# Stick-breaking attention: block C taken head by head, block B's high part moved to VectorE, and some steps of the memory attention put elsewhere

## The chip, the core and the metric

The kernel runs on one core of a Trainium2 chip. The core has five engines with instruction queues of their own: TensorE (PE: matmuls, with PEld for its weight loads), VectorE (DVE), ScalarE (ACT), GpSimd (POOL) and SyncE (SP, which issues the DMAs). They meet only through semaphores. The metric is the device time of one execution in microseconds, and lower is better. Each engine works through its own list in order, so an instruction that waits holds up all that stand behind it on its engine.

## The reference

A streaming encoder with two layers over 512 tokens of width 1024, all in float32. Layer 0 has a half SwiGLU block, a mixer of gated spatial weights and a memory cross-attention of four heads, and a second half SwiGLU block. Layer 1 has the same blocks, but its mixer is stick-breaking attention over a shared K and V (12 heads of 64) beside the memory cross-attention. The change is in the two mixers. Stick-breaking attention in the reference, cut to the core:

```python
z = einsum('bqhd,bkhd->bhqk', qi, k) * scale
causal = key_pos < qpos
log_beta = log_sigmoid(z)
log_one_minus = where(causal, log_sigmoid(-z), 0.0)
suffix = cumsum(log_one_minus, reverse=True) - log_one_minus   # over the keys
a = where(causal, exp(log_beta + suffix), 0.0)
out = einsum('bhqk,bkhd->bqhd', a, v)
```

Memory cross-attention is plain softmax attention over 256 memory rows, four heads of 64.

## The kernel before

Every float32 product is made of three matmuls in a fast number format: each operand is split into a high part (a rounded copy, written by ScalarE or VectorE) and a low part (what the rounding lost, a subtraction, mostly on GpSimd). Names end in `_hi` and `_lo`. All weights stream through two buffers: SyncE loads `raw`, ScalarE writes `w_hi`, GpSimd writes `w_lo`, TensorE multiplies. One such piece of weights is a unit (`unit_T`, `unit_N`, `unit_wide`).

The kernel has no scheduler. The order on each engine is the order of the code, written by hand in five blocks, one for each engine. Small steps that don't use the weight stream are put between the matmuls of a unit as its `steps`: `unit_T` runs step 0 after two of its eight k-chunks, step 1 after four, step 2 after six and step 3 at the end. The memory attention runs in this way. For each head h there are `mem_scores`, `mem_transposes` and `mem_values` on TensorE, and `mem_steps` says which stands where.

The stick-breaking attention of layer 1 goes over six pairs of heads (`PAIRS`, index c). Keys lie on partitions and queries along the columns, in blocks of 128 keys. These are grouped in three: A holds key blocks 1 and 3, B holds block 2, C holds block 0. A and C have 2 x 512 columns for the two heads of a pair, B has 2 x 256. For each of A, B and C of a pair the work is a chain through all engines:

1. TensorE: the dots z (`sb_scores_a`, `_b`, `_c`), with the causal mask.
2. VectorE: the absolute value (`sb_abs`) into `sp_l`. ScalarE: `sb_exp` and `sb_log` in place, log(1 + exp(-|z|)). VectorE: `sb_plus` adds max(z, 0). This is the softplus of z.
3. The high part `sp_hi` (`sb_high`, on VectorE for A and C; `sb_high_b`, on ScalarE, for B from pair 1 on), then the low part `sp_lo` on GpSimd (`sb_low`, `lows_after`).
4. TensorE: the sums over later keys, as matmuls with a triangle (`tri_r`) or minus ones (`minus_r`), added to z in the same PSUM bank (`sb_sums_a_high`, `sb_sums_a_low`, `sb_sums_b`, `sb_sums_b_on_a`, `sb_sums_c`).
5. ScalarE: `sb_out`, the exponential, which gives the weights `aT`. TensorE: `sb_values` multiplies them with V; then `sb_y` splits the result into `y_hi` and `y_lo`.

The chains of several pairs overlap. TensorE in round c (the body of its loop for pair c) runs the sums of A and B of pair c, the values of pair c-1 around the scores of B of pair c+1, the sums of C of pair c, the scores of C of pair c+1 and the scores of A of pair c+2. PSUM is full: the scores of A of pair c+2 go into the banks of C of pair c, and so wait for its `aT_c` (`s_a[C_]`). The scores of B of pair c+1 use the one bank of B and wait for `aT_b` of pair c (`s_a[B_]`). `sp_hi_c` and `sp_lo_c` have one buffer each; those of A and B have two. The last pair's sums of C and its values run as steps of the output projection.

The semaphores that the change touches are `s_sp`, `s_sphi`, `s_splo`, `s_tri` (the sums of a block are complete) and `s_a`.

## Time and profile before

| | before |
|---|---|
| median of 3 runs | 1857.85 us (1857.71 to 1858.12) |
| the profiled execution | 1858.24 us |
| its span in the trace | 1856.5 us |
| TensorE busy | 1848.3 us |
| GpSimd, VectorE, ScalarE busy | 902.7, 842.1, 639.9 us |
| granted TensorE clock | full speed in all 40 slices |

The span is the time between the first and the last instruction of the trace; the time of an execution is a little longer. Busy times count the time in which an engine had an instruction at work. The attention over the six pairs lies between about 1364 and 1448 us of the span; the memory attention of layer 0 between about 415 and 456 us, and that of layer 1 between about 1339 and 1383 us.

### The profile page before, as it was taken

What the parts mean: (1) busy time and instruction counts of PE and PEld (TensorE: products, weight loads), DVE (VectorE), ACT (ScalarE), POOL (GpSimd) and SP (SyncE); (2) the same over time, 40 slices, a digit from 0 to 9 for tenths busy, and PEclk for the clock granted to TensorE, in tenths of its full rate; (3) what the DMA queues carried; (4) which work ended last, traced back from release to release, by engine and by line L of the source; (5) the groups of instructions that cost most, each with busy time, mean ns of one, the idle gap of its engine ahead of it and who ended that gap; (6) DMA issues with size and microseconds to landing.
All of it is one profiled execution on the core that took longest, in us unless ns stands there. A gap on an engine that the chain in (4) does not pass through costs nothing.

```text
span 1856.5 us, 22737 instructions
## 1 busy us (share of the span) xinstructions
PE 1848.3 (100%) x8640; PEld 1527.7 (82%) x8640; DVE 842.1 (45%) x723; ACT 639.9 (34%) x894; POOL 902.7 (49%) x433
## 2 busy tenths in 40 slices
PE   9999999999999999999999999999999999999999
PEld 7888888897888888888888888888877888888887
DVE  7442154554555520554435530444667455502543
ACT  6432232336443221323333222223568333222223
POOL 5444444563444544444545444544658445444542
PEclk9999999999999999999999999999999999999999
DMA  6223322352232234223322223222310232233222
GB/s 205 91 83 96 115 90 67 114 171 74 69 112 92 85 85 125 90 74 96 124 92 90 93 82 119 91 87 82 107 65 1 75 107 90 75 106 113 90 71 88
DMA packets 215981, 175.56 MB, mean 95 GB/s; under 512 B 3247, under 2 KB 212989, under 8 KB 215933
## 3 DMA queue, kind: packets, MB, share of 16 engines
q1 hardware_dynamic: 215932, 174.90, 30.2%
q8 instruction: 32, 0.52, 0.1%
q14 instruction: 17, 0.13, 0.0%
HBM read 172.79 MB, written 2.10 MB: 94 GB/s over the span
## 4 chain that ended last, share of the span: by engine, by line
PE 98%; ACT 1%; DVE 0%; DMA 0%; POOL 0%; issue 0%; SPq 0%; ACTq 0%
PE ps L591 31%; PE ps L592 31%; PE ps L593 31%; PE ps L899 1%; PE ps L1016 1%; PE ps L663 1%; PE ps L690 1%; PE ps L892 1%; PE ps L860 0%; PE ps L872 0%; PE ps L881 0%; PE ps L1073 0%; DMA x_in<-in_x_dram 0%; ACT aT_c L1508 0%; PE ps L794 0%; PE ps L1160 0%
## 5 line engine op out<-in xcount | busy, mean ns | idle before, releaser
L483 POOL TENSOR_TENSOR w_lo<-raw,w_hi 128x1024 fp32r<-128x1024 f32 (+2 forms) x360 | 824.9, 2312 | 908.6 <-ACT w_hi L1221 908.6
L1221 ACT ACTIVATE w_hi<-raw 128x1024 fp32r<-128x1024 f32 (+2 forms) x361 | 328.6, 958 | 1097.8 <-PE ps L593 1089.9
L591 PE MATMUL ps<-u_hi,w_hi 128*128 128x512 f32 x1568 | 612.3, 390 | 0.0
L592 PE MATMUL ps<-u_lo,w_hi 128*128 128x512 f32 x1568 | 610.8, 390 | 0.0
L593 PE MATMUL ps<-u_hi,w_lo 128*128 128x512 f32 x1568 | 610.7, 389 | 0.0
L591 PEld LDWEIGHTS ps<-u_hi,w_hi 128*128 128x128 f32 x1568 | 294.4, 188 | 61.9 <-issue 0.6
L593 PEld LDWEIGHTS ps<-u_hi,w_lo 128*128 128x128 f32 x1568 | 294.4, 188 | 61.4
L592 PEld LDWEIGHTS ps<-u_lo,w_hi 128*128 128x128 f32 x1568 | 294.5, 188 | 60.6 <-issue 0.2
L591 PE MATMUL ps<-mid_hi,w_hi 128*128 128x512 f32 (+1 forms) x714 | 276.2, 387 | 0.0
L593 PE MATMUL ps<-mid_hi,w_lo 128*128 128x512 f32 (+1 forms) x714 | 275.9, 386 | 0.0
L592 PE MATMUL ps<-mid_lo,w_hi 128*128 128x512 f32 (+1 forms) x714 | 275.9, 386 | 0.0
L1584 DVE TENSOR_TENSOR mid_lo<-t_mid,mid_hi 128x512 f32 (+1 forms) x88 | 176.9, 2049 | 54.1 <-ACT mid_hi L1275 54.1
L1584 DVE TENSOR_TENSOR t_up<-t_gate,rinv 128x512 f32<-128x512 f32 x88 | 166.2, 1927 | 57.2 <-ACT t_gate L1268 57.2
L1721 DVE SCALAR_TENSOR_TENSOR xT<-ps,xT 128x512 f32 (+1 forms) x63 | 43.6, 692 | 276.5 <-PE ps L593 276.5
L592 PEld LDWEIGHTS ps<-mid_lo,w_hi 128*128 128x128 f32 x714 | 134.1, 188 | 27.1
L593 PEld LDWEIGHTS ps<-mid_hi,w_lo 128*128 128x128 f32 x714 | 134.1, 188 | 27.0
L591 PEld LDWEIGHTS ps<-mid_hi,w_hi 128*128 128x128 f32 x714 | 134.1, 188 | 26.9
L1584 DVE TENSOR_TENSOR t_gate<-ps,rinv 128x512 f32<-128x512 f32 (+1 forms) x89 | 58.9, 703 | 194.1 <-PE ps L593 194.1
L1584 DVE TENSOR_TENSOR t_mid<-ps,t_up 128x512 f32<-128x512 f32 x88 | 56.7, 686 | 178.1 <-PE ps L593 177.7
L1584 DVE TENSOR_TENSOR ssq<-ssq,sq 128x512 f32<-128x512 f32 x52 | 99.8, 1920 | 12.7 <-ACT sq L1251 12.2
L1590 DVE SCALAR_TENSOR_TENSOR u_lo<-xT,gains,u_hi (+1 forms) x40 | 39.5, 986 | 48.3 <-ACT u_hi L1249 48.3
L1268 ACT ACTIVATE t_gate<-t_gate 128x512 f32<-128x512 f32 x88 | 50.1, 616 | 11.3 <-DVE t_gate L1584 11.3
(252 smaller groups left out, 1363.6 us busy)
## 6 DMA issues: line engine op xcount, KB each, us to landing
raw<-in_ffn_w_up_dram SPq DMA_DIRECT2D x44, 1024.0 KB, 5.3
raw<-in_ffn_w_gate_dram SPq DMA_DIRECT2D x43, 1024.0 KB, 5.3
raw<-in_ffn_w_down_dram SPq DMA_DIRECT2D x32, 768.0 KB, 4.8
raw<-in_ffn_w_down_dram SPq DMA_DIRECT2D x32, 640.0 KB, 4.4
raw<-in_a_w_in_dram SPq DMA_DIRECT2D x7, 1024.0 KB, 5.3
raw<-in_w_kv_dram SPq DMA_DIRECT2D x6, 1024.0 KB, 5.0
raw<-in_a_w_out_dram SPq DMA_DIRECT2D x4, 1024.0 KB, 5.1
raw<-in_b_w_in_dram SPq DMA_DIRECT2D x4, 1024.0 KB, 5.4
```

The costliest lines, as they stand in the source:

```text
L483: nc.gpsimd.tensor_tensor(w_lo[:, n % 2, part], raw[:, n % 2, part], w_hi[:, n % 2, part].bitcast(F32), ALU.subtract).then_inc(s_wlo, 1)
L591: nc.tensor.matmul(dst, s_hi, m_hi_, start=first, stop=False)
L592: nc.tensor.matmul(dst, s_hi, m_lo_, start=False, stop=False)
L593: return nc.tensor.matmul(dst, s_lo, m_hi_, start=False, stop=last)
L663: last = nc.tensor.matmul(dst, o[:, k, toks], w[:, k, :], start=k == 0 and t % 2 == 0 and term == 0, stop=k == DK - 1 and term == 2, skip_ ...
L690: last = nc.tensor.matmul(ps[:, bank(0) + c, :], w[:, k, c * P:(c + 1) * P], u[:, k, :], start=k == 0 and w is wh and u is u_hi, stop=k == ...
L892: last = nc.tensor.matmul(dst, w[rows_, c, j * P:(j + 1) * P], m[rows_, m_k, j * P:], start=first and w is k_hi and m is q_hi, stop=False, ...
L1221: nc.scalar.activation(w_hi[:, n % 2, part], raw[:, n % 2, part], ACT.Copy).then_inc(s_whi, 1)
L1268: nc.scalar.activation(t_gate[:, q, :], t_gate[:, q, :], ACT.Silu).then_inc(s_silu, 1)
L1584: return nc.vector.tensor_tensor(dst, x, y, op)
L1590: nc.vector.scalar_tensor_tensor(u_lo[:, bass.ds(i + k, 1), :], xT[:, bass.ds(i + k, 1), :], gains[:, bass.ds(i + (gain + k), 1)], u_hi[:, ...
L1721: nc.vector.scalar_tensor_tensor(x_k, ps[:, bank(n):bank(n) + 1, :], 0.5, x_k, ALU.mult, ALU.add).then_inc(s_evac, 1)
```

## The change

Stick-breaking attention, block C:
- `sb_plus` and `sb_high` of C become `sb_plus_and_high_c`, which takes head 0 and then head 1, 512 columns each. `sb_low_c` does the same for the low part. `s_sp`, `s_sphi` and `s_splo` of C count to two for each pair.
- `sb_sums_c` runs the triangle matmuls as high and low of head 0, then high and low of head 1, with a new semaphore `s_tri_c0` for head 0. It waits for both heads' `s_sp` at its start.
- `sb_out_c` takes the exponential of head 0 after `s_tri_c0` and that of head 1 after `s_tri`.

Block B: its logarithm (`sb_log`) moves behind `sb_out_c` on ScalarE. Its high part moves from ScalarE to VectorE for all pairs, and stands there between `sb_plus(B_)` and `sb_abs(C_)`.

Values of pair 4 (`c == PAIRS - 2`): the wait for `aT_c` moves from the start of `sb_values` to block C's matmuls, the last of the four.

Memory attention: `mem_scores` of head 1 moves by one slot, to stand directly before the transposes of head 0, in both layers. In layer 0 the transposes of the spatial weights follow the values of head 3 directly, mixes 0 and 1 run two k-chunks later in their unit, mixes 2 and 3 directly behind them (so in the unit before their old one), and mixes 4 and 5 stay.

```diff
@@ gpsimd
+            def sb_low_c(c):
+                for e in range(2):
+                    pool.wait_ge(s_sphi[C_], 2 * c + e + 1)
+                    nc.gpsimd.tensor_tensor(sp_lo[C_][c % 2][:, e, :], sp_l[C_][:, e, :],
+                                            sp_hi[C_][c % 2][:, e, :].bitcast(F32),
+                                            ALU.subtract).then_inc(s_splo[C_], 1)
@@ tensor
             def sb_sums_c(c):
-                pe.wait_ge(s_sp[C_], c + 1)
+                pe.wait_ge(s_sp[C_], 2 * c + 2)
...
-                pe.wait_ge(s_sphi[C_], c + 1)
-                for e in range(2):
+                for e, done in enumerate((s_tri_c0, s_tri[C_])):
+                    pe.wait_ge(s_sphi[C_], 2 * c + e + 1)
                     add_high(z[:, e, :], tri_r[:], C_, c, e, WHOLE)
-                pe.wait_ge(s_splo[C_], c + 1)
-                for e in range(2):
-                    last = add_low(z[:, e, :], tri_r[:], C_, c, e, WHOLE)
-                last.then_inc(s_tri[C_], 1)
+                    pe.wait_ge(s_splo[C_], 2 * c + e + 1)
+                    add_low(z[:, e, :], tri_r[:], C_, c, e, WHOLE).then_inc(done, 1)
 
             def sb_values(c, blocks):
                 first, end = (1, 0) if c == PAIRS - 2 else (0, TT - 1)
-                for x in (A_, B_, C_):
+                for x in (A_, B_) if c == PAIRS - 2 else (A_, B_, C_):
                     pe.wait_ge(s_a[x], c + 1)
...
+                    if c == PAIRS - 2 and x == C_:
+                        pe.wait_ge(s_a[x], c + 1)
@@ mem_steps
-                        scores(1), transposes(0), both(values(0), scores(2)), transposes(1),
+                        nothing, both(scores(1), transposes(0)), both(values(0), scores(2)), transposes(1),
@@ layer 0
-            unit_T(n + 4, ... steps=(lambda: mem_values(0, 3), spatial_weights, nothing, nothing))
-            unit_T(n + 5, ... steps=(nothing, mixes(0), nothing, nothing))
-            unit_T(n + 6, ... steps=(nothing, mixes(2), nothing, mixes(4)))
+            unit_T(n + 4, ... steps=(values_and_weights, nothing, nothing, nothing))
+            unit_T(n + 5, ... steps=(nothing, nothing, lambda: mixes(range(4)), nothing))
+            unit_T(n + 6, ... steps=(nothing, nothing, nothing, lambda: mixes(range(4, GK))))
@@ scalar
-            def sb_high_b(c):
...
+            def sb_out_c(c):
+                if c:
+                    act.wait_ge(s_bv, c)
+                for e, ready in enumerate((s_tri_c0, s_tri[C_])):
+                    act.wait_ge(ready, c + 1)
+                    last = nc.scalar.activation(aT[C_][c % 2][:, e, :], ps_of(C_, c)[:, e, :], ACT.Exp)
+                last.then_inc(s_a[C_], 1)
...
                     sb_exp(B_, c + 1)
-                    sb_log(B_, c + 1)
...
-                sb_out(C_, c)
+                sb_out_c(c)
                 if more:
-                    sb_high_b(c + 1)
+                    sb_log(B_, c + 1)
                     sb_exp(C_, c + 1)
                     sb_log(C_, c + 1)
@@ vector
+            def sb_plus_and_high_c(c):
+                dve.wait_ge(s_ln[C_], c + 1)
+                for e in range(2):
+                    nc.vector.scalar_tensor_tensor(sp_l[C_][:, e, :], ps_of(C_, c)[:, e, :], 0.0, sp_l[C_][:, e, :],
+                                                   ALU.max, ALU.add).then_inc(s_sp[C_], 1)
+                    dve.wait_ge(s_sp[C_], 2 * c + e + 1)
+                    if c:
+                        dve.wait_ge(s_tri[C_], c)
+                    nc.vector.tensor_copy(sp_hi[C_][c % 2][:, e, :], sp_l[C_][:, e, :]).then_inc(s_sphi[C_], 1)
...
-                sb_plus(C_, c)
-                sb_high(C_, c)
+                sb_plus_and_high_c(c)
...
                     sb_plus(B_, c + 1)
+                    sb_high(B_, c + 1)
                     sb_abs(C_, c + 1)
```

ScalarE's list around the exponential of block C, pair 2, before. The first `sp_l_b` is the exponential of B of pair 3 and the second its logarithm; the numbers behind the names tell two buffers of one name apart, and the semaphores waited for stand in brackets:

```order
L1508 ACTIVATE aT_a_126<-ps 128x1024 [waits s_bv,s_tri_a]
L1495 ACTIVATE sp_l_b<-sp_l_b 128x512 [waits s_abs_b]
L1500 ACTIVATE sp_l_b<-sp_l_b 128x512 [waits s_em_b]
L1508 ACTIVATE aT_c_130<-ps 128x1024 [waits s_bv,s_tri_c]
L1515 ACTIVATE sp_hi_b_117<-sp_l_b 128x512 [waits s_tri_c,s_sp_b]
L1495 ACTIVATE sp_l_c<-sp_l_c 128x1024 [waits s_abs_c]
L1500 ACTIVATE sp_l_c<-sp_l_c 128x1024 [waits s_em_c]
L1508 ACTIVATE aT_b_129<-ps 128x512 [waits s_bv,s_tri_b]
```

The same place in the changed kernel:

```order
L1522 ACTIVATE aT_a_126<-ps 128x1024 [waits s_bv,s_tri_a]
L1509 ACTIVATE sp_l_b<-sp_l_b 128x512 [waits s_abs_b]
L1530 ACTIVATE aT_c_130<-ps 128x512 [waits s_tri_c0,s_bv]
L1530 ACTIVATE aT_c_130<-ps 128x512 [waits s_tri_c]
L1514 ACTIVATE sp_l_b<-sp_l_b 128x512 [waits s_em_b]
L1509 ACTIVATE sp_l_c<-sp_l_c 128x1024 [waits s_abs_c]
L1514 ACTIVATE sp_l_c<-sp_l_c 128x1024 [waits s_em_c]
L1522 ACTIVATE aT_b_129<-ps 128x512 [waits s_bv,s_tri_b]
```

The logarithm of B has moved behind `aT_c`, which is now two instructions, and the copy `sp_hi_b` is gone from ScalarE.

VectorE's list from the high part of A of pair 2 to the absolute value of B of pair 3, before:

```order
L1952 CAST sp_hi_a_114<-sp_l_a 128x1024 [waits s_tri_c,s_sp_a]
L1584 TENSOR_TENSOR y_lo<-ps,y_hi 128x512 [waits s_byhi]
L1943 SCALAR_TENSOR_TENSOR sp_l_b<-ps,sp_l_b 128x512 [waits s_ln_b]
L1937 TENSOR_SCALAR sp_l_c<-ps 128x1024 [waits s_splo_c,s_z_c]
L1937 TENSOR_SCALAR sp_l_a<-ps 128x1024 [waits s_splo_a,s_z_a]
L1943 SCALAR_TENSOR_TENSOR sp_l_c<-ps,sp_l_c 128x1024 [waits s_ln_c]
L1952 CAST sp_hi_c_118<-sp_l_c 128x1024 [waits s_tri_c,s_sp_c]
L1937 TENSOR_SCALAR sp_l_b<-ps 128x512 [waits s_splo_b,s_z_b]
```

The same stretch in the changed kernel:

```order
L1966 CAST sp_hi_a_114<-sp_l_a 128x1024 [waits s_tri_c,s_sp_a]
L1599 TENSOR_TENSOR y_lo<-ps,y_hi 128x512 [waits s_byhi]
L1958 SCALAR_TENSOR_TENSOR sp_l_b<-ps,sp_l_b 128x512 [waits s_ln_b]
L1966 CAST sp_hi_b_116<-sp_l_b 128x512 [waits s_tri_c,s_sp_b]
L1952 TENSOR_SCALAR sp_l_c<-ps 128x1024 [waits s_splo_c,s_z_c]
L1952 TENSOR_SCALAR sp_l_a<-ps 128x1024 [waits s_splo_a,s_z_a]
L1972 SCALAR_TENSOR_TENSOR sp_l_c<-ps,sp_l_c 128x512 [waits s_ln_c]
L1977 CAST sp_hi_c_118<-sp_l_c 128x512 [waits s_tri_c,s_sp_c]
L1972 SCALAR_TENSOR_TENSOR sp_l_c<-ps,sp_l_c 128x512
L1977 CAST sp_hi_c_118<-sp_l_c 128x512 [waits s_tri_c,s_sp_c]
L1952 TENSOR_SCALAR sp_l_b<-ps 128x512 [waits s_splo_b,s_z_b]
```

The cast of B is new between B's sum and C's absolute value, and the sum and cast of C are each in two halves that alternate.

## Rows read from the trace of the kernel before

**Rows 1.** The page's part 1: each engine's busy time and instructions.
```profile
PE 1848.3 (100%) x8640; PEld 1527.7 (82%) x8640; DVE 842.1 (45%) x723; ACT 639.9 (34%) x894; POOL 902.7 (49%) x433
```
**Rows 2.** Busy times by window, memory attention of both layers: window, length, engines, clock.
```profile
414.00:500.00 86.00, 85.96 (x480) 70.12 (x479) 41.56 (x44) 45.00 (x81) 30.50 (x12) 1.00 0.26 83
1338.00:1372.00 34.00, 34.00 (x209) 26.59 (x208) 17.03 (x17) 18.67 (x46) 20.36 (x8) 1.00 0.25 82
```
**Rows 3.** The same view of rounds 2 and 3 (PE, PEld, DVE, ACT, POOL).
```profile
1400.71:1411.63 10.92, 10.86 (x71) 7.82 (x71) 8.56 (x10) 9.04 (x11) 8.71 (x8) 1.00 0.01 2
1411.63:1422.54 10.91, 10.84 (x71) 7.83 (x71) 8.56 (x10) 9.02 (x11) 8.70 (x8) 1.00 0.00 0
```
**Rows 4.** Waits: who waited for whom, us in total, times, longest.
```profile
PEld ps L892 <- ACT aT_c L1508: 2.0, 4, 0.5
...
PE ps L899 <- POOL sp_lo_c L505: 0.7, 1, 0.7
...
PE ps L1016 <- ACT aT_c L1508: 0.3, 1, 0.3
```
**Rows 5.** Timeline of TensorE, round 4: start, duration, instruction, count.
```profile
1422.07 0.40 PE L892 MATMUL ps<-q_lo_rest,k_hi 64*128 64x512 f32 x2
1422.54 0.44 PE L892 MATMUL ps<-q_hi,k_hi 64*128 64x384 f32 x2
...
1427.50 0.38 PE L892 MATMUL ps<-q_hi,k_hi 64*128 64x256 f32 x1
...
1431.25 0.62 PE L899 MATMUL ps<-sp_hi_c,tri_r 128*128 128x512 f32 x2
```
**Rows 6.** Timeline of ScalarE, from B's logarithm to `aT_b` and A's exponential.
```profile
1420.94 0.64 ACT L1500 ACTIVATE sp_l_b<-sp_l_b 128x512 f32<-128x512 f32 x1
1421.48 1.00 ACT L1508 ACTIVATE aT_c<-ps 128x1024 f32<-128x1024 f32 x1
...
1423.81 1.06 ACT L1495 ACTIVATE sp_l_c<-sp_l_c 128x1024 f32<-128x1024 f32 x1 [0.50 <-DVE sp_l_c L1937]
1424.90 1.06 ACT L1500 ACTIVATE sp_l_c<-sp_l_c 128x1024 f32<-128x1024 f32 x1
1425.96 0.60 ACT L1508 ACTIVATE aT_b<-ps 128x512 f32<-128x512 f32 x1
1426.45 1.05 ACT L1495 ACTIVATE sp_l_a<-sp_l_a 128x1024 f32<-128x1024 f32 x1
```
**Rows 7.** Chain of what ended last, pair 0's block C: start, duration, what.
```profile
1383.47 1.23 DVE sp_l_c L1943
1384.73 0.70 DVE sp_hi_c L1952
1385.50 2.39 POOL sp_lo_c L505
1387.94 0.75 PE ps L899 x2
```
**Rows 8.** Timelines of VectorE and GpSimd: casts of 512 columns, and GpSimd's work.
```profile
1379.21 0.92 DVE L1952 CAST sp_hi_b<-sp_l_b 128x512 fp32r<-128x512 f32 x1
...
543.69 0.43 DVE L1600 CAST ssq_hi<-ssq 128x512 fp32r<-128x512 f32 x1
...
1377.45 2.39 POOL L505 TENSOR_TENSOR sp_lo_a<-sp_l_a,sp_hi_a 128x1024 fp32r<-128x1024 f32 x1 [6.43 <-DVE sp_hi_a L1952]
...
1383.48 1.28 POOL L557 TENSOR_TENSOR lo<-sp_lo_a,lo 128x512 fp32r<-128x512 f32 x1
```
**Rows 9.** Timelines of VectorE and GpSimd, round 3.
```profile
1421.96 0.68 DVE L1943 SCALAR_TENSOR_TENSOR sp_l_b<-ps,sp_l_b 128x512 f32<-128x512 f32 x1
1422.56 1.22 DVE L1937 TENSOR_SCALAR sp_l_c<-ps 128x1024 int32<-128x1024 int32 x1
...
1421.52 2.39 POOL L505 TENSOR_TENSOR sp_lo_a<-sp_l_a,sp_hi_a 128x1024 fp32r<-128x1024 f32 x1 [1.45 <-DVE sp_hi_a L1952]
```
**Rows 10.** Chain of what ended last, layer 0: scores of memory head 1.
```profile
422.16 0.90 PE ps L860 x12
```

More of the change, by code:

```diff
@@ L307, in trunk_program @@
         s_zb0 = sem("s_zb0")
+        s_tri_c0 = sem("s_tri_c0")
         s_lo23, s_lo123 = sem("s_lo23"), sem("s_lo123")
@@ L563, in _ @@
             for c in range(PAIRS):
-                sb_low(C_, c)
+                sb_low_c(c)
                 if c + 1 < PAIRS:
@@ L1081, in _, with values_and_weights, mixes @@
             unit_wide(n + 2, u_hi, u_lo, steps=steps[4:])
-            unit_T(n + 4, 0, u_hi, u_lo, steps=(lambda: mem_values(0, 3), spatial_weights, nothing, nothing))
-            def mixes(g):
-                return lambda: (mix(g), mix(g + 1))
-            unit_T(n + 5, 0, u_hi, u_lo, steps=(nothing, mixes(0), nothing, nothing))
-            unit_T(n + 6, 0, u_hi, u_lo, steps=(nothing, mixes(2), nothing, mixes(4)))
+            def values_and_weights():
+                mem_values(0, MH - 1)
+                spatial_weights()
+            unit_T(n + 4, 0, u_hi, u_lo, steps=(values_and_weights, nothing, nothing, nothing))
+            def mixes(groups):
+                for g in groups:
+                    mix(g)
+            unit_T(n + 5, 0, u_hi, u_lo, steps=(nothing, nothing, lambda: mixes(range(4)), nothing))
+            unit_T(n + 6, 0, u_hi, u_lo, steps=(nothing, nothing, nothing, lambda: mixes(range(4, GK))))
             def y_ready_a(k):
@@ L1508, in sb_out @@
                 nc.scalar.activation(aT[x][c % 2][:], ps_of(x, c), ACT.Exp).then_inc(s_a[x], 1)
-            def sb_high_b(c):
-                act.wait_ge(s_sp[B_], c + 1)
-                if c > 1:
-                    act.wait_ge(s_tri[C_], c - 1)
-                nc.scalar.activation(sp_hi[B_][c % 2][:], sp_l[B_][:], ACT.Copy).then_inc(s_sphi[B_], 1)
+            def sb_out_c(c):
[5 more added lines that the diff above has]
+                last.then_inc(s_a[C_], 1)
             def sb_y(c):
@@ L1935, in sb_abs @@
                 if c:
-                    dve.wait_ge(s_splo[x], c)
+                    dve.wait_ge(s_splo[x], 2 * c if x == C_ else c)
                 nc.vector.tensor_scalar(sp_l[x][:].bitcast(I32), ps_of(x, c).bitcast(I32), 0x7FFFFFFF, None,
@@ L1948, in sb_high @@
                 dve.wait_ge(s_sp[x], c + 1)
-                used = c if x == C_ else c - 1
-                if used > 0:
-                    dve.wait_ge(s_tri[C_], used)
+                if c > 1:
+                    dve.wait_ge(s_tri[C_], c - 1)
                 nc.vector.tensor_copy(sp_hi[x][c % 2][:], sp_l[x][:]).then_inc(s_sphi[x], 1)
+            def sb_plus_and_high_c(c):
[7 more added lines that the diff above has]
+                    nc.vector.tensor_copy(sp_hi[C_][c % 2][:, e, :], sp_l[C_][:, e, :]).then_inc(s_sphi[C_], 1)
             def sb_y(c):
```

## The prediction, as made before the changed kernel was run

> **What bounds the kernel now.** The page is read first. TensorE is busy for 1848.3 of 1856.5 us, VectorE for 842.1, ScalarE for 639.9 and GpSimd for 902.7 [rows 1]. Every microsecond of TensorE is therefore on the path, and work on the other three costs nothing until TensorE waits for it. The change touches two stretches. In the memory attention of both layers TensorE is busy for 85.96 of 86 us and for all of 34 us [rows 2], so nothing is there to win: the scores and transposes only change places in it. The other stretch is the stick-breaking loop, a few us in each of five rounds. A round takes 10.92 us, of which VectorE works 8.6, ScalarE 9.0 and GpSimd 8.7 [rows 3]: three helpers at four fifths, which hand data to each other in a fixed order.
>
> The list of waits comes next, and it names all that the change can win [rows 4]. Once TensorE waits 0.7 us for the low half of block C's softplus (pair 0). Four times the weight load of `sb_scores_a` waits for `aT_c`, 2.0 us by the list; but a load normally runs ahead of its matmul, so the cost is smaller. The matmul rows give it: the last group of block C's dots starts at 1422.07 and the next at 1422.54, 0.47 us later, where its 512 columns take 0.23 [rows 5]. So each of these stalls costs 0.24 us. Last, `sb_values(4)` waits 0.3 us for the same `aT_c`. Together 0.7 + 4 x 0.24 + 0.3 = 1.9 us, 0.1% of the time.
>
> **The change, part by part.**
>
> *Block C's exponential by head.* TensorE now finishes head 0 (its high and low matmul) before it starts head 1, so ScalarE starts 0.46 us earlier. A 512-column exponential holds ScalarE for 0.49 us (1425.96 to 1426.45) and takes 0.60; the 1024-column one takes 1.00 [rows 6]. The end moves from 1.00 after the last sum to 0.6, which is 0.4 earlier and more than the stall of 0.24. The matmuls are as many as before, of the same size. Alone, this would remove the stalls in rounds 1 to 4.
>
> *Block C's softplus and high part by head, pair 0.* Now: sum 1383.47, cast 1384.73, subtraction 1385.50 for 2.39 us, matmul 1387.94 [rows 7]. What matters is how a VectorE cast meets GpSimd. A cast of 512 columns alone takes 0.43 us. At 1379.21 the cast of `sp_hi_b` took 0.92: GpSimd had been on `sp_lo_a` since 1377.45 for 2.39 us, to 1379.84, and the cast ended at 1380.13, 0.29 later [rows 8]. So it stood still until GpSimd's instruction was over. Applied to pair 0: sum of head 0 to 1384.15; its cast waits for GpSimd's `lo` (1383.48 to 1384.76, rows 8), ends 1385.05; subtraction of head 0 at 1385.12 to 1386.41 (GpSimd takes 1.28 for 512 columns, rows 8); sum of head 1 ends 1385.65 (`sb_sums_c` now waits for it first, within the same stall); its cast stands until 1386.41 and ends at 1386.70; subtraction of head 1 ends at 1388.06; matmul at 1388.12. Only one 0.23 matmul is left then instead of two, so it is done at 1388.35 against 1388.40 now. Gain: nothing. The 0.7 us stall stays, since the casts and subtractions of the two heads cannot overlap.
>
> *The logarithm of block B behind `aT_c`, its cast on VectorE.* This makes a loop through all engines that did not bind before. I count from the moment when TensorE has finished head 0 of block C of one round. Exponentials of both heads: 0.07 to start, 0.49 each: 1.05. Logarithm of B 0.63: 1.68 [rows 6]. VectorE's sum for B 0.68: 2.39, cast ready to start at 2.42 [rows 9]. Where is GpSimd? The subtraction `sp_lo_a` starts 1.20 us after TensorE began the high sums of block C (1421.52 against 1420.32, the latter being 1431.25 less one round of 10.93), which is 0.58 on my clock, and lasts 2.39: to 2.97 [rows 5, 9]. The cast of B stands behind it and ends at 3.26. Behind the cast in VectorE's order waits the absolute value of block C of the next pair, which now runs at 1422.56, straight behind B's sum [rows 9]. It starts at 3.2, ends at 4.40. Exponential of C 4.43, logarithm 1.09 later, 5.52; `aT_b` 6.5 (it followed 1.06 behind the logarithm, where it may have waited a little; I take 1.0), 0.60 long: 7.1; TensorE may start `sb_scores_b` at 7.2 [rows 6]. From that start to head 0's end TensorE needs 1431.25 - 1427.50 = 3.75, plus 0.23 and 0.39: 4.37 [rows 5]. The loop is 7.2 + 4.35 = 11.55 us, against 10.92 now: 0.63 a round. The new wait is `sb_scores_b` for `aT_b`; today it has almost 1 us to spare (ready 1426.56, used 1427.50 [rows 5, 6]). Queued behind it on ScalarE are A's exponential and logarithm, which move back by the same time but are needed only 3 us later.
>
> ScalarE's cast of B (about 0.6 us) goes away; it is worth nothing, since the loop's delay is on VectorE.
>
> The Trainium skill, "SBUF — State Buffer", section "Who interferes with whom", says that copy, cast and tensor_scalar can all take the port pair that VectorE shares with GpSimd, and that the second to come is blocked wholly. For the cast the trace agrees (0.92 against 0.43). For the absolute value, a tensor_scalar out of PSUM, it does not: it took 1.22 at 1422.56 in the midst of `sp_lo_a`, as elsewhere. By the rule read so widely C's absolute value would stand behind `sp_lo_b` too, and the round would be over 12.5 us; the row decides, and I leave it out.
>
> *First round and pair 1.* The same walk from pair 0: head 1 of C ends at 1388.5, ScalarE's second half at 1389.06, logarithm of B to 1389.69, sum to 1390.40; `sp_lo_a` now runs 1389.23 to 1391.62, so the cast ends 1391.9, C's absolute value 1393.05, `aT_b` 1395.74, `sb_scores_b` 1395.80. Now it starts at 1394.74 (1427.50 less three rounds of 10.92 [rows 3, 5]); the cost is 1.1 us. Pair 1 also carries `query_rest_low(1)`, a VectorE subtraction with both inputs in SBUF, in the same crowded place. No row shows it there behind a blocked cast: between 0 and 0.7 us (its own length), I take 0.3.
>
> *Values of pair 4 per block.* Blocks A and B go first and hide `aT_c`: the stall of 0.3 goes, and so does the 0.24 in the last `sb_scores_a`, as the loop has made ScalarE early there.
>
> *Memory scores beside transposes; mixes and spatial weights moved.* Same matmuls, two to three us earlier or later in weights work without a wait. Scores of head 1 take 0.90 [rows 10]; what follows them (maximum, exponential) must wait for the transposes of head 0 in any case, because both use `pm`. I price this at 0, with 0.1 us on either side for each of the four places, a tenth of a 0.9 us step.
>
> **Sum.** 1.1 + 3 x 0.63 + 0.3 - 0.5 = 2.8 us. The profiled execution took 1858.24 us with its span of 1856.5; with 2.8 more that is 1861.0. The median of the runs is 0.39 lower, so the forecast for it is 1860.6.
>
> **Rivals.**
> *It does what it says.* The stalls of 1.9 us go and nothing new comes: 1856.0. For it: ScalarE and VectorE have over 2 us free in a round. Against it: that spare time lies elsewhere than between B's logarithm and C's absolute value, and the casts stand. Chance 0.13.
> *The cast of B does not stand.* If A's subtraction is over or not yet begun when B's cast comes, the cast takes 0.43 from 2.42, and C's absolute value starts at 2.8 instead of 3.2: a loop of 11.15 us, 0.2 a round. With a first round at no cost and 0.5 won at the end, the sum is about zero: 1857.8. Chance 0.15.
> *GpSimd becomes the bound, clearly slower.* Its halves cost 2 x 1.29 for 2.39, and each cast of block C waits for the half before it. This pushes A's absolute value, sum and subtraction back too. It decides from the point where the second half of C ends later than TensorE asks for it (in round 0 it does). Then `sp_lo_a` and `sp_lo_b` come late and the round is 12.1 us: 4 x 1.2 - 0.5 = 4.3 us, 1862.2. Chance 0.14.
> *Forecast*: chance 0.58, own range 1859.3 to 1861.7.
>
> **How the numbers follow.** Range 1857.2 to 1862.2: below it lies the first rival (0.13), above it half of the third (0.07). About 0.2%, 3.7 us, is what a measurement of this kernel can tell from no change. Faster by that needs 1854.1, more than all stalls together: 0.01. Slower by that needs 1861.6: most of the third rival and the forecast's upper end, 0.17. The rest, 0.82, is within.
>
> **What would show it.** In the changed profile: casts of `sp_hi_b` of 0.7 to 1.5 us that end 0.29 after `sp_lo_a`; C's absolute value more than 2.5 us behind head 0's end; TensorE waiting for `aT_b` (line of `sb_dots`) in rounds 1 to 4; rounds of about 11.5 us; the wait at 1387 still there; no wait for `aT_c` in `sb_scores_a` or `sb_values`; the two memory stretches as long as before. I am wrong if the rounds are at or under 10.9 us, or if B's casts take 0.43.

## The result and the profile after

| | before | after |
|---|---|---|
| median of 20 runs each | 1857.86 us (1857.57 to 1860.01) | 1860.57 us (1860.18 to 1861.53) |
| profiled execution, span | 1858.24, 1856.5 us | 1860.19, 1858.5 us |

The ratio is 1.0015, with a 95% interval of 1.0009 to 1.0021: the change costs 2.7 us, and 1860.6 had been forecast. Engine times hardly moved, as the page's part 1 of the changed kernel shows beside [rows 1]:

```profile
PE 1849.3 (100%) x8640; PEld 1526.9 (82%) x8640; DVE 849.9 (46%) x740; ACT 636.2 (34%) x895; POOL 904.4 (49%) x439
```

TensorE's busy time rose by 1.0 us and the span by 2.0, so the shares of busy time don't tell where the time went. The list of waits of the changed kernel (attention stretch; who waited for whom, us in total, times, longest) answers to [rows 4]:

```profile
PEld ps L901 <- ACT aT_b L1522: 3.8, 4, 1.0
PEld ps L908 <- POOL sp_lo_b L506: 2.2, 4, 0.7
PE ps L908 <- POOL sp_lo_b L506: 1.4, 4, 0.4
...
PE ps L901 <- ACT aT_b L1522: 1.1, 4, 0.3
...
PEld ps L901 <- ACT aT_c L1530: 0.5, 3, 0.2
...
PEld ps L908 <- DVE sp_l_c L1972: 0.3, 1, 0.3
PE ps L908 <- POOL sp_lo_c L513: 0.3, 1, 0.3
```

The stalls for `aT_c` are nearly gone (2.0 us to 0.5, and none in the values). Two new ones took their place: TensorE waits for B's low part and then for `aT_b`, once in each of the four rounds. One round in the timeline of the changed kernel (VectorE, GpSimd, ScalarE; start, duration), to be held beside [rows 6, 9]:

```profile
1411.19 1.09 ACT L1530 ACTIVATE aT_c<-ps 128x512 f32<-128x512 f32 x2
...
1411.66 2.40 POOL L506 TENSOR_TENSOR sp_lo_a<-sp_l_a,sp_hi_a 128x1024 fp32r<-128x1024 f32 x1 [1.27 <-DVE sp_hi_a L1966]
1412.16 0.63 ACT L1514 ACTIVATE sp_l_b<-sp_l_b 128x512 f32<-128x512 f32 x1
...
1412.82 0.69 DVE L1958 SCALAR_TENSOR_TENSOR sp_l_b<-ps,sp_l_b 128x512 f32<-128x512 f32 x1 [0.64 <-ACT sp_l_b L1514]
...
1413.55 0.79 DVE L1966 CAST sp_hi_b<-sp_l_b 128x512 fp32r<-128x512 f32 x1
...
1414.26 1.21 DVE L1952 TENSOR_SCALAR sp_l_c<-ps 128x1024 int32<-128x1024 int32 x1
...
1415.51 1.06 ACT L1509 ACTIVATE sp_l_c<-sp_l_c 128x1024 f32<-128x1024 f32 x1 [2.72 <-DVE sp_l_c L1952]
...
1416.60 1.06 ACT L1514 ACTIVATE sp_l_c<-sp_l_c 128x1024 f32<-128x1024 f32 x1
...
1417.56 0.58 ACT L1522 ACTIVATE aT_b<-ps 128x512 f32<-128x512 f32 x1
...
1418.19 0.18 PEld L901 LDWEIGHTS ps<-q_hi,k_hi 64*128 64x128 f32 x1 [0.96 <-ACT aT_b L1522]
```

`sp_lo_a` ends at 1414.06 and the cast at 1414.34. C's absolute value starts behind it, 1.44 us after B's sum began; it was 0.60 [rows 9]. ScalarE idles 2.72 us in front of C's exponential.

**A ruler for the rest.** Start-up differs by up to 1.3 us from one profiled execution to the next (the sums of squares in layer 0 start 25.5 to 26.8 us behind the first matmul, whatever the kernel). In the profiled execution of the changed kernel TensorE came to the attention 1.0 us earlier than in that of the kernel before, which is why the spans differ by 2.0 us and the attention by 3.0. So the traces are compared by lengths inside the attention: from the start of TensorE's first matmul of `sp_hi_c` of one pair to that of the next ("rounds" 0 to 4), and from the start of the first matmul of `q_hi,k_hi` to that of the last of `aT_c` ("attention"). What lies before round 0 and behind round 4 is in "attention" alone. The times are the medians.

| kernel | round 0, 1, 2, 3, 4 | attention | time |
|---|---|---|---|
| before | 11.88 10.93 10.91 10.93 11.08 | 82.37 | 1857.85 to 1858.02 |
| after | 12.54 11.96 11.48 11.47 10.73 | 85.33 | 1860.57 |
| 1 memory steps alone | 11.90 10.92 10.91 10.92 11.07 | 82.36 | 1857.49 |
| 2 C by head alone | 11.80 11.14 10.98 10.99 11.14 | 83.05 | 1858.55 |
| 3 after, B's high part on ScalarE | 11.80 11.50 10.98 10.97 10.74 | 83.01 | 1858.18 |
| 4 after, B's logarithm first | 12.55 11.95 11.47 11.48 10.75 | 85.34 | 1860.54 |
| 5 B's high part on VectorE alone | 12.20 11.47 11.47 11.47 11.08 | 84.58 | 1860.13 |
| 6 C's exponential by head alone | 11.82 10.97 10.99 10.98 11.14 | 82.53 | 1858.36 |
| 7 after, B's high part without a cast | 11.85 11.46 11.37 11.37 10.73 | 83.87 | 1859.01 |
| 8 first candidate | 11.68 10.98 10.98 10.98 10.74 | 83.71 | 1858.67 |
| 9 memory steps and values | 11.89 10.93 10.92 10.91 10.74 | 82.02 | 1857.13 |
| 10 B's high part behind C's absolute value | 12.02 11.14 11.15 11.14 11.07 | 83.15 | 1858.71 |
| 11 as 6, B's logarithm behind | 12.13 11.24 10.98 10.97 10.74 | 82.81 | 1858.27 |
| 12 as 8, sums wait by head | 11.17 10.97 10.97 10.97 10.73 | 81.97 | 1857.06 |

Each experiment's time is a median of 11 runs; the kernel before ran beside them, 1858.02, 1857.93, 1857.85 and 1857.87 us in the four sets (1 to 4, 5 to 8, 9 to 11, 12). The intervals of the ratios are about 0.0009 wide on either side. So by the medians alone only the changed kernel and experiments 4 and 5 are slower for certain, and differences under 1.7 us rest on the rounds.

### The profile page after: what moved, and what is told of

It reads as the page before. It is cut to its first block, busy times and chain, and to the rows that moved or that the text cites. A ratio compares the mean times of both kernels' runs of the same rounds, so it can differ in the third digit from the quotient of the medians.

```text
span 1858.5 us, 22765 instructions
## 1 busy us (share of the span) xinstructions
PE 1849.3 (100%) x8640; PEld 1526.9 (82%) x8640; DVE 849.9 (46%) x740; ACT 636.2 (34%) x895; POOL 904.4 (49%) x439
## 4 chain that ended last, share of the span: by engine, by line
PE 97%; DVE 1%; ACT 1%; POOL 1%; issue 1%; DVEq 0%; POOLq 0%
PE ps L600 31%; PE ps L601 31%; PE ps L602 31%; PE ps L672 1%; PE ps L699 1%; POOL sp_lo_a L506 1%; PE ps L908 0%; PE ps L869 0%; PE ps L1025 0%; PE ps L881 0%; DVE sp_l_c L1952 0%; PE ps L890 0%; DVE sp_l_a L1958 0%; PE ps L1082 0%; ACT sp_l_c L1509 0%
```

## The experiments

**1. The memory steps alone.**

```diff
-                        scores(1), transposes(0), both(values(0), scores(2)), transposes(1),
+                        nothing, both(scores(1), transposes(0)), both(values(0), scores(2)), transposes(1),
...
+            unit_T(n + 4, 0, u_hi, u_lo, steps=(values_and_weights, nothing, nothing, nothing))
```

> The kernel before with the changes to the memory attention and the mixes alone; the stick-breaking part is as before. My prediction (priced at nothing): 0.0 us, within 0.1 for each of the four places. What the start times of the matmuls in the changed kernel's trace say instead: -0.1 us at the memory attention of layer 0, -0.1 at the mixes, -0.1 at the memory attention of layer 1, -0.35 together, so a median of 1857.5 against 1857.9. If TensorE's list around these steps has a cost when it goes back and forth between them and the weight matmuls, the gain stays; if it was chance, the three places show no shift.

1857.49 beside 1858.02 us; ratio 0.9998 (0.9989 to 1.0007). Counted from the sums of squares in layer 0, TensorE gains 0.13 us over the memory scores of layer 0, 0.10 over its values and mixes, and 0.12 in layer 1: 0.35, with the attention as long as before. The gain is real, and the changed kernel has the same one: from the sums of squares to the attention it is 1336.56 to 1336.62 us in the eight traces with these steps and 1336.92 to 1336.95 in the six without. Part of where it comes from shows in the chain (start, duration, line; L591 to L593 are the weight matmuls, L860 the scores, L872 the transposes). Before:

```profile
423.06 0.43 PE ps L591
...
426.05 0.87 PE ps L872 x8
426.93 0.23 PE ps L591
```

With scores and transposes beside each other:

```profile
424.46 0.90 PE ps L860 x12
425.36 1.02 PE ps L872 x8
426.38 0.23 PE ps L591
```

The weight matmul behind the scores took 0.43 us and takes 0.23 elsewhere; the transposes behind the scores take 1.02 for 0.87. That is 0.05 of the 0.13; where the rest is, these rows don't tell.

**2. Block C by head alone**, with B as before.

```diff
 # on the kernel before
+                    add_high(z[:, e, :], tri_r[:], C_, c, e, WHOLE)
+                    pe.wait_ge(s_splo[C_], 2 * c + e + 1)
+                    add_low(z[:, e, :], tri_r[:], C_, c, e, WHOLE).then_inc(done, 1)
...
+                sb_plus_and_high_c(c)      # VectorE
+                sb_low_c(c)                # GpSimd
+                sb_out_c(c)                # ScalarE
```

> The kernel before with block C by head alone (softplus, high and low part, sums, exponential); block B's logarithm stays ahead of aT_c and its high part on ScalarE; pair 4's values and the memory steps as before. Theory (the loop through B's cast is the cost): most of the change's +3.0 us in the attention is absent here; left is a later round 0 and the blocked second cast, about +1.0 us, rounds of 10.9 to 11.1. Rival (GpSimd's and VectorE's halves are the cost): +2 us or more, with rounds of over 11.3. Rival (it does what it says): -1 to -2 us.

1858.55 us, ratio 1.0003 (0.9994 to 1.0012); attention +0.68. The rounds are 10.98 to 11.14, so GpSimd's halves are not the bound. But nothing is gained either: TensorE's weight loads still wait 2.1 us for `aT_c`. C's cast of head 0 stands behind GpSimd in four of the six pairs, for 1.53 to 1.55 us.

**3. The changed kernel with B's high part back on ScalarE.**

```diff
                     sb_log(B_, c + 1)
+                    sb_high_b(c + 1)
...
                     sb_plus(B_, c + 1)
-                    sb_high(B_, c + 1)
```

> The changed kernel with block B's high part back on ScalarE, directly behind B's logarithm (which stays behind aT_c). Theory (the cast of B on VectorE stands until GpSimd's sp_lo_a ends and pushes C's absolute value): C's absolute value starts straight behind B's sum again, rounds fall from 11.5 to 11.0 or less, and the time from 1860.6 to about 1858.1 (+0.2 to +0.5 over before). Rival (the late logarithm of B is the cost): 1860 or more, and the wait of sb_scores_b for aT_b stays at over 0.3 us a round.

1858.18 us, ratio 1.0001 (0.9992 to 1.0010); attention 83.01, which gives back 2.32 of the 2.96 us. C's absolute value starts at 1412.88, 0.61 behind the start of B's sum (1412.27), and rounds 2 and 3 are 10.98 and 10.97. Most of the cost is thus the cast on VectorE; round 1 stays at 11.50, for 10.93 before.

**4. The changed kernel with B's logarithm first.**

```diff
                     sb_exp(B_, c + 1)
+                    sb_log(B_, c + 1)
...
-                    sb_log(B_, c + 1)
                     sb_exp(C_, c + 1)
```

> The changed kernel with block B's logarithm back ahead of aT_c; its high part stays on VectorE. Theory (the blocked cast): B's sum comes earlier but its cast ends with sp_lo_a all the same, so C's absolute value is no earlier: within 0.3 us of the changed kernel, 1860.6, rounds of 11.4 to 11.5. Rival (the late logarithm of B is the cost, two thirds of the loop's delay): 1858.5, rounds of 11.0.

1860.54 us, ratio 1.0014 (1.0005 to 1.0023), and every round within 0.02 us of the changed kernel's. In this kernel it is nothing that the logarithm stands behind `aT_c`.

**5. B's high part on VectorE alone.** On the kernel before:

```diff
-                    sb_high_b(c + 1)
...
                     sb_plus(B_, c + 1)
+                    sb_high(B_, c + 1)
                     sb_abs(C_, c + 1)
```

> The kernel before with one edit: block B's high part on VectorE between B's sum and C's absolute value, from ScalarE. Theory (this cast stands until GpSimd's sp_lo_a ends and holds C's absolute value back): this edit alone costs most of the change's 2.95 us in the attention, about +2.4 us: 1860.3, rounds of about 11.4, and sb_scores_b waits for aT_b. Rival (the cost needs block C by head or the late logarithm of B beside it): under +1 us, 1858.9 or less.

1860.13 us, ratio 1.0013 (1.0004 to 1.0022); attention +2.21. Rounds 2 and 3 are 11.47, the same as in the changed kernel to 0.01; rounds 0 and 1 are 0.34 and 0.49 shorter than there. Its timeline:

```profile
1411.13 2.39 POOL L505 TENSOR_TENSOR sp_lo_a<-sp_l_a,sp_hi_a 128x1024 fp32r<-128x1024 f32 x1 [1.01 <-DVE sp_hi_a L1944]
1411.57 0.68 DVE L1935 SCALAR_TENSOR_TENSOR sp_l_b<-ps,sp_l_b 128x512 f32<-128x512 f32 x1
...
1412.29 1.52 DVE L1944 CAST sp_hi_b<-sp_l_b 128x512 fp32r<-128x512 f32 x1
1413.73 1.21 DVE L1929 TENSOR_SCALAR sp_l_c<-ps 128x1024 int32<-128x1024 int32 x1
```

The cast begins 1.16 us behind the start of `sp_lo_a`, where it was 1.89 in the changed kernel, takes 1.52 for 0.79, and ends 0.29 after `sp_lo_a` (1413.81, 1413.52), for 0.28 there. Where a cast stands behind GpSimd, its own start is worth nothing; GpSimd's end decides. That is also why experiment 4 showed no difference.

**6. C's exponential by head alone**, softplus and parts whole.

```diff
+                for e, done in enumerate((s_tri_c0, s_tri[C_])):
+                    pe.wait_ge(s_sphi[C_], c + 1)
+                    add_high(z[:, e, :], tri_r[:], C_, c, e, WHOLE)
+                    pe.wait_ge(s_splo[C_], c + 1)
+                    add_low(z[:, e, :], tri_r[:], C_, c, e, WHOLE).then_inc(done, 1)
...
+                sb_out_c(c)
```

> The kernel before with block C's sums and exponential by head alone; its softplus, high and low part stay whole. My prediction said that this alone removes the four stalls of sb_scores_a for aT_c (-1.0 us: 1857.0), since ScalarE starts 0.46 us earlier. Rival, by the rows before: ScalarE is not free earlier, as B's exponential and logarithm stand ahead (the logarithm ends at 1421.47, and aT_c starts at 1421.48); two exponentials of 512 then end 0.05 to 0.1 later than one of 1024, and the stalls stay at 0.5 us in the list: +0.2 to +0.3 us, 1858.2.

1858.36 us, ratio 1.0001 (0.9992 to 1.0010); attention +0.16. The rival holds. ScalarE's timeline here:

```profile
1420.98 0.62 ACT L1494 ACTIVATE sp_l_b<-sp_l_b 128x512 f32<-128x512 f32 x1
1421.63 0.63 ACT L1499 ACTIVATE sp_l_b<-sp_l_b 128x512 f32<-128x512 f32 x1
1422.17 1.06 ACT L1515 ACTIVATE aT_c<-ps 128x512 f32<-128x512 f32 x2
```

`aT_c` starts when B's logarithm is done, as before, and its two halves take 1.06 us for 1.00.

**7. B's high part without a cast.** In the changed kernel VectorE writes it with the operation of the sum, out of PSUM.

```diff
+                nc.vector.scalar_tensor_tensor(sp_hi[B_][c % 2][:], ps_of(B_, c), 0.0, sp_l[B_][:], ALU.max,
+                                               ALU.add).then_inc(s_sphi[B_], 1)
+                dve.wait_ge(s_sphi[B_], c + 1)
                 nc.vector.scalar_tensor_tensor(sp_l[B_][:], ps_of(B_, c), 0.0, sp_l[B_][:], ALU.max,
                                                ALU.add).then_inc(s_sp[B_], 1)
```

> The changed kernel, where block B's high part is written on VectorE by the operation of its sum (max(z, 0) + l, z out of PSUM, rounded on writing) and not by a cast; the sum itself follows it, and GpSimd and TensorE wait for both. VectorE so does 0.68 us where the cast took 0.43, but the operation is of a kind that did not stand behind GpSimd in the trace. Theory (the cast stands because of what it reads and writes, not because it is one more instruction): both take 0.68 each, in the midst of sp_lo_a too; C's absolute value starts earlier and the rounds are 11.1: about 1858.8. Rival (any added instruction there costs as much, or this one stands too): 1860.6 or more.

1859.01 us, ratio 1.0007 (0.9998 to 1.0016); attention 83.87, 1.46 less than the changed kernel's. Its timeline:

```profile
1410.93 2.41 POOL L508 TENSOR_TENSOR sp_lo_a<-sp_l_a,sp_hi_a 128x1024 fp32r<-128x1024 f32 x1 [1.16 <-DVE sp_hi_a L1969]
...
1411.91 0.69 DVE L1976 SCALAR_TENSOR_TENSOR sp_hi_b<-ps,sp_l_b 128x512 fp32r<-128x512 f32 x1 [0.46 <-ACT sp_l_b L1517]
1412.63 0.69 DVE L1979 SCALAR_TENSOR_TENSOR sp_l_b<-ps,sp_l_b 128x512 f32<-128x512 f32 x1
1413.24 1.21 DVE L1955 TENSOR_SCALAR sp_l_c<-ps 128x1024 int32<-128x1024 int32 x1
```

Two operations of 0.69 us pass within `sp_lo_a`, neither held. What stood in the changed kernel was the cast from SBUF to SBUF, not an added instruction as such. Kind of operation and source were changed together here, so which of the two decides is not shown. Rounds 2 and 3 fall only to 11.37 where 11.1 was expected, since a second 0.69 us takes the place of most of the stall; 1.2 of the 1.46 us come from rounds 0 and 1.

**8. A candidate**: experiment 3, with C's high parts written in the manner of 7.

```diff
+                    nc.vector.scalar_tensor_tensor(sp_hi[C_][c % 2][:, e, :], ps_of(C_, c)[:, e, :], 0.0,
+                                                   sp_l[C_][:, e, :], ALU.max, ALU.add).then_inc(s_sphi[C_], 1)
+                    dve.wait_ge(s_sphi[C_], 2 * c + e + 1)
                     nc.vector.scalar_tensor_tensor(sp_l[C_][:, e, :], ps_of(C_, c)[:, e, :], 0.0, sp_l[C_][:, e, :],
```

> The changed kernel with two edits: block B's high part back on ScalarE behind B's logarithm, and block C's high parts written by the operation of the sum out of PSUM (high, then sum, for each head; GpSimd waits for both), so that no cast of 512 columns is left that GpSimd's subtraction of the other head can hold up. Theory: the second head's high part no longer stands behind the subtraction of the first, C's low part ends earlier, the wait of pair 0 shrinks and the stalls for aT_c go: attention -1.2 us against the kernel before, with the memory steps 1856.4. Rival (the longer operations on VectorE, 0.25 us each, take back what they give): 1857.5 to 1858.

1858.67 us, ratio 1.0001 (0.9992 to 1.0010); attention +1.34, not -1.2. A miss, and most of it is in pair 0: the first `sp_hi_c` matmul comes 24.11 us into the attention, for 22.39 before, while rounds 0 to 4 together are only 0.4 us shorter. Its row in the waits, and its windows (length; busy PE, PEld, DVE, ACT, POOL; granted clock):

```profile
PE ps L909 <- DVE sp_l_c L1986: 0.7, 1, 0.7
```

```profile
1384.00:1385.00 1.00, 0.75 (x4) 0.42 (x4) 0.97 (x3) 0.97 (x2) 0.80 (x1) 1.00 0.00 0
1385.00:1386.00 1.00, 0.57 (x4) 0.57 (x4) 1.00 (x3) 1.00 (x3) 0.96 (x2) 0.88 0.00 0
1386.00:1387.00 1.00, 1.00 (x6) 1.00 (x6) 1.00 (x1) 0.83 (x2) 0.81 (x1) 0.50 0.00 0
...
1388.00:1389.00 1.00, 1.00 (x4) 0.81 (x3) 0.17 (x1) 0.42 (x1) 1.00 (x1) 0.50 0.00 0
```

TensorE waits 0.7 us for C's last sum, ahead of all the minus-one sums, and behind this wait its clock is granted at 0.50 (1.2 GHz) for some 3 us. The triangle matmuls of 512 columns follow each other every 0.43 us there, for 0.23. The eleven times lie in two groups, 1857.2 to 1857.8 (four) and 1858.2 to 1859.0 (seven). The mean granted clock of the run is 0.999 in six of the seven, the profiled one among them, and 1.000 in the four and in the seventh, 1858.24; some 3 us at 0.50 make 0.001 of the span. That the clock fell here only in the second group is therefore likely, but only the profiled run, 1858.73, shows where it fell.

In the kernel before, TensorE waits as long in pair 0 (0.7 us for the low part), and the clock stays at 1.00:

```profile
1387.00:1388.00 1.00, 0.29 (x2) 0.06 (x1) 0.97 (x2) 0.97 (x3) 0.89 (x1) 1.00 0.00 0
1388.00:1389.00 1.00, 1.00 (x6) 0.84 (x8) 1.00 (x3) 0.62 (x2) 0.48 (x1) 1.00 0.00 0
```

**9. Memory steps and pair 4's values.**

```diff
-                for x in (A_, B_, C_):
+                for x in (A_, B_) if c == PAIRS - 2 else (A_, B_, C_):
...
+                    if c == PAIRS - 2 and x == C_:
+                        pe.wait_ge(s_a[x], c + 1)
```

> The kernel before with the two parts of the change that nothing spoke against: the memory steps and mixes (0.37 us in the first experiment), and pair 4's values that wait per block (the wait of 0.3 us in the list, 0.28 by the loop as it was). Theory: the two add up: -0.65 us, 1857.3, and it beats both kernels. Rival (the wait of pair 4's values only moves to the next instruction that needs ScalarE or the sums of pair 5): 1857.6.

1857.13 us (1856.92 to 1857.66) beside 1857.85 (1857.53 to 1858.76); ratio 0.9996 (0.9987 to 1.0005). It is 0.7 us faster, as expected, and its ranges nearly don't meet, though the interval of the ratio doesn't exclude no change. In the trace round 4 is 0.34 shorter, and the wait of the values for `aT_c` is gone from the list.

**10. B's high part on VectorE, behind C's absolute value.**

```diff
                     sb_plus(B_, c + 1)
                     sb_abs(C_, c + 1)
+                    sb_high(B_, c + 1)
```

> As the experiment with block B's high part alone on VectorE (1860.1, +2.2 us), but behind C's absolute value and no longer ahead of it. The cast stays on VectorE and may still stand behind GpSimd. Theory (the price is that C's absolute value is queued behind the standing cast): C's absolute value starts straight behind B's sum, the rounds are 10.9 to 11.0 and the time is 1857.9 to 1858.2. Rival (the price is the late high and low part of B itself, or VectorE's added work): 1859.5 or more, for B's high part comes later still.

1858.71 us, ratio 1.0006 (0.9997 to 1.0015); attention +0.78, between the two. C's absolute value starts at once and B's cast is short; C's cast is the longer one:

```profile
1410.90 0.68 DVE L1935 SCALAR_TENSOR_TENSOR sp_l_b<-ps,sp_l_b 128x512 f32<-128x512 f32 x1
...
1411.50 1.21 DVE L1929 TENSOR_SCALAR sp_l_c<-ps 128x1024 int32<-128x1024 int32 x1
1412.63 0.52 DVE L1944 CAST sp_hi_b<-sp_l_b 128x512 fp32r<-128x512 f32 x1
...
1416.05 1.28 POOL L557 TENSOR_TENSOR lo<-sp_lo_a,lo 128x512 fp32r<-128x512 f32 x1
1416.19 1.68 DVE L1944 CAST sp_hi_c<-sp_l_c 128x1024 fp32r<-128x1024 f32 x1
```

So 1.4 of the 2.2 us of experiment 5 are what was queued behind the cast. The other 0.8 is the recorded rival's late low part of B. B's cast still ends 0.29 us after `sp_lo_a`, so `sp_lo_b` starts later, and TensorE waits for it:

```profile
1413.22 1.31 POOL L505 TENSOR_TENSOR sp_lo_b<-sp_l_b,sp_hi_b 128x512 fp32r<-128x512 f32 x1 [0.37 <-DVE sp_hi_b L1944]
...
1414.58 0.19 PEld L899 LDWEIGHTS ps<-sp_lo_b,tri_r 128*128 128x128 f32 x1 [0.19 <-POOL sp_lo_b L505]
```

The same two of the kernel before, where the round begins 0.15 us later (1409.42, here 1409.27):

```profile
1412.98 1.29 POOL L505 TENSOR_TENSOR sp_lo_b<-sp_l_b,sp_hi_b 128x512 fp32r<-128x512 f32 x1
...
1414.47 0.19 PEld L899 LDWEIGHTS ps<-sp_lo_b,tri_r 128*128 128x128 f32 x1
```

From the round's start `sp_lo_b` begins 0.39 us later (3.95 for 3.56), its weight load 0.26 (5.31 for 5.05), and the round is 11.15 for 10.91. C's own cast is no new stall: it took 1.27 us before, and ends 0.55 after GpSimd's `lo` in both.

**11. As 6, with B's logarithm behind `aT_c`**, B's high part on ScalarE.

```diff
                     sb_exp(B_, c + 1)
-                    sb_log(B_, c + 1)
...
+                    sb_log(B_, c + 1)
                     sb_high_b(c + 1)
```

> As the experiment with block C's sums and exponential by head alone (1858.4), and block B's logarithm moved behind aT_c, its high part still on ScalarE behind it. Theory (exponential by head gains only where ScalarE is free when head 0 is complete): the waits of sb_scores_a for aT_c, 2.1 us in the list before, go; instead TensorE waits for B's low part, about 0.15 us a round; rounds of 10.9, the attention 0 to 0.3 us shorter than in the kernel before: 1857.6 to 1857.9. Rival (the stalls for aT_c stay, because the second head's exponential ends no earlier): 1858.4 or more.

1858.27 us, ratio 1.0002 (0.9993 to 1.0011); attention +0.44. The stalls for `aT_c` go (2.0 us before and 1.7 in 6, to 0.3), so exponential by head needs the freed ScalarE. But rounds 2 and 3 are 10.98 and 10.97, no shorter. The waits moved:

```profile
PEld ps L893 <- ACT aT_b L1507: 2.4, 4, 0.6
PEld ps L900 <- POOL sp_lo_c L506: 1.9, 3, 1.3
PEld ps L900 <- POOL sp_lo_b L506: 1.3, 4, 0.4
```

Of these only the last is a new cost in rounds 2 and 3. The load in front of `sb_scores_b` idles 0.60 us a round in the kernel before too, where the list calls it "issue", and 1.3 us of the second line is the stall of pair 0, 1.1 there. The second half of the expectation was wrong: in rounds 2 and 3 TensorE waits for B's late low part as much as it gains, and in rounds 0 and 1 the kernel takes 0.3 us more each than that of 6 (12.13 and 11.24 for 11.82 and 10.97).

**12. The candidate with the wait for C's sums by head.**

```diff
-                pe.wait_ge(s_sp[C_], 2 * c + 2)
                 z = ps_of(C_, c)
                 for e in range(2):
+                    pe.wait_ge(s_sp[C_], 2 * c + e + 1)
```

> The candidate of before (B's high part on ScalarE, C's high parts by the operation of the sum), where TensorE waits for the sum of each head of C ahead of that head's minus-one sums, and no longer for both heads at the start. In the candidate's profile TensorE's granted clock fell to 0.50 (1.2 GHz) behind the wait of pair 0, from 1385.9 to 1389.1, and its times lay in two groups (4 runs from 1857.2 to 1857.8, 7 from 1858.2 to 1859.0). Theory (that wait, and the low clock behind it, are the whole miss): head 0's sums fill the wait, the clock stays at 1.00 and all runs lie about 1857.2, the attention at about 82.2. Rival (the rounds of 10.98 and the longer work on VectorE cost as much as was won): about 1857.5 with the clock at 1.00, the attention at 82.5 or more; or the wait is only split in two, and the clock falls again: 1858.5.

1857.06 us (1856.87 to 1857.69) beside 1857.87 (1857.72 to 1858.45), ratio 0.9996 (0.9987 to 1.0005); attention 81.97, 0.40 shorter than before. The theory's numbers hold: with the wait split the clock stays at 1.00 there, and 1.74 of the attention's microseconds come back. How much of them is the wait and how much the clock, this pair of runs doesn't tell. It was not the whole miss of 8, which had expected -1.2. The same stretch:

```profile
1385.00:1386.00 1.00, 0.68 (x4) 0.69 (x5) 1.00 (x3) 1.00 (x3) 0.96 (x2) 1.00 0.00 0
1386.00:1387.00 1.00, 1.00 (x6) 0.79 (x6) 0.99 (x1) 0.89 (x3) 0.71 (x1) 1.00 0.00 0
```

With 9 it is the fastest kernel here; all its 11 times lie under those of the kernel before beside them. It wins the stall of pair 0 (round 0: 11.17 for 11.88, though its first `sp_hi_c` matmul comes 22.91 us into the attention for 22.39) and the values' wait (0.34), and pays 0.05 in each of rounds 1 to 3. Experiment 9, with the memory steps and the values' wait alone, is within 0.05 us of it in the attention (82.02).

## Why the prediction was right

*The loop.* It failed nowhere. From the start of `aT_c` (1411.19, 0.07 on the prediction's clock) the changed kernel has B's cast end at 3.22 (forecast 3.26), C's absolute value at 3.14 (3.2; it starts while the cast ends), C's exponential at 4.39 (4.43), its logarithm at 5.48 (5.52), `aT_b` at 6.44 (6.5) and `sb_scores_b` at 7.07 (7.2). The round is 11.47, not 11.55: `sb_scores_b` came 0.13 early, half of it in the last step (0.63 us, where 0.7 had been taken), and from there to head 0's end it is 4.40, where the sum has 4.35 and its own working 4.37. The cause is shown both ways, by adding the cast (5) and by taking it away (3), and its kind by 7.

*First round and pair 1.* `sb_scores_b` of pair 2 starts at 1394.75, and TensorE came to the attention 1.01 us earlier than before, so it lost 1.02 against 1394.74; 1.1 was forecast. From there to its start for pair 3 are 11.97 us, then 11.47 and 11.48: +1.05, +0.55, +0.56 to 10.92, forecast 0.93, 0.63, 0.63. `query_rest_low`, put at 0.3, is thus nearer 0.5. By the timeline it costs this together with C's halves, which leave VectorE no idle time up to A's high part: `sp_lo_a` starts 1.67 us after the first `sp_hi_c` matmul (1.20 in the next round), and B's cast ends with it. In experiment 5, without the halves, the same subtraction costs nothing (11.47, as in the rounds behind it). The parts tried alone don't add up: 2.21 (5) + 0.68 (2) - 0.35 (9) is 2.54 of 2.96. By the table, rounds 0 and 1 lose 0.7 more than the parts together and the rest 0.3 less; beyond `query_rest_low`, by which wait it comes stays open.

*Pair 0.* Its gain was put at nothing, since cast and subtraction of the two heads can't overlap. TensorE comes 0.36 later to `sp_hi_c` (it waits 0.3 for both sums), and then waits 0.3 instead of 0.7 for the low part.

*Exponential by head.* The sentence "Alone, this would remove the stalls in rounds 1 to 4" was wrong (6: 10.97 to 10.99 for 10.91 to 10.93). It counted from TensorE's end of head 0, and left out that B's logarithm holds ScalarE from 1420.94 to 1421.58, and that `aT_c` starts straight behind it, at 1421.48 [rows 6]. In the changed kernel the logarithm had moved, so the sum was not touched.

*Pair 4's values.* The step that failed. Forecast was -0.5 behind the last `sb_scores_b`, of which 0.3 for the wait and 0.24 for the last `sb_scores_a`. Measured is 2.96 - 1.02 - 1.05 - 0.55 - 0.56: -0.2. The wait alone gives -0.35 (9). The 0.24 was counted twice: the last `sb_scores_a` stands ahead of the last `sb_scores_b`, inside a round whose length the loop sets. And 0.14 us is lost behind the last `sp_hi_c` (4.39 us to the end of the attention, for 4.25): the weight load of pair 5's last low part waits 0.3 us for GpSimd, since C's chain of pair 5 comes late by the loop. The halves are not the cause: with them and without B's cast on VectorE it is 4.25 and 4.26 (2, 3), and with the cast and without the halves 4.50 (5). Nor is the gain of 0.35 the edit's alone in this kernel: round 4 is 10.74 in experiment 11 too, without the edit, since `aT_c` is ready earlier there.

*Memory steps.* Priced at 0 within 0.1 for each place; they give 0.35 in three places, where the two stretches were to be "as long as before". This makes up, by luck, for what the term before lacked, and the sum of 2.8 met 2.7 partly for that reason: the attention's 2.96 less 0.35 is 2.61.

*Rivals.* "The cast of B does not stand": it did, in all five rounds (0.77 to 1.37 us). GpSimd as the bound: not with rounds of 10.98 (2, 3). "It does what it says": even without the cast rounds 2 and 3 close again at 10.97 to 10.99 (2, 3, 11).

## What to carry to other kernels

Before a cast from SBUF to SBUF is moved to VectorE, look at what GpSimd does at that moment and at what is queued behind the cast: here it ended by GpSimd's instruction, not by its own length, and starting it earlier brought nothing. What waits for the cast's own result is late too (10). When an exponential or another consumer is split so that it may start earlier, read the engine's own list first: if it is busy until the old start, the split only adds overhead (6). Where several engines at four fifths close a loop, count the round and not the wait: a stall that was removed came back as a wait for another engine in experiments 3, 11 and 12.

## What the runs showed of the hardware

- A cast from SBUF to SBUF of 512 columns behind GpSimd took up to 1.80 us for 0.43 (4, pair 1), one of 1024 columns 1.27 in the kernel before and 1.68 in 10, for 0.69. B's ended 0.28 to 0.29 after GpSimd's instruction, whenever they began, and C's of 1024 columns 0.55 after. So these two engines don't meet only through semaphores. A scalar_tensor_tensor with one input in PSUM kept its 0.69 us under the same GpSimd instruction. The Trainium skill, "SBUF — State Buffer", section "Who interferes with whom", says that an instruction with at most one SBUF input, outside the two-port modes, does not contend; the trace agrees (0.69, and 1.21 for the absolute value out of PSUM). The absolute value has no input in SBUF, so the prediction's row of 1.22 us does not speak against that section, as the prediction had it.
- It works the other way round too. In the changed kernel the subtraction `q_lo_rest`, both of whose inputs lie in SBUF, starts at 1396.97 on VectorE and takes its usual 0.68 us; GpSimd's `sp_lo_c` of 512 columns, begun 0.16 later, takes 1.67 us for 1.28.
- Behind one wait of 0.7 us TensorE's clock was granted at 0.50 (1.2 GHz) for 3 us (8). Behind an equal wait in the kernel before it stayed at 1.00. What sets them apart, these runs don't show.
- The weight matmul behind the memory scores (64 rows of weights) took 0.43 us for 0.23, and transposes behind them 1.02 for 0.87.
